# Two layer ends reordered: squares of the last tile summed second, first root turned early, first weight chunks in halves

## What is computed

```
h = _rmsnorm(x, pre_g) * (1 + scale) + shift
proj = h @ w_in
...
x = x + gate * _rmsnorm(y @ w_out, post_g)
```

## Time and profile before

| what | value |
| --- | --- |
| device time, median of 3 runs | 2637.5 us (2636.26 to 2640.43) |
| the profiled execution's own time | 2639.43 us |
| its span | 2637.6 us |
| TensorE's mean granted clock | 0.981 of full |
| instructions | 31436 |
| DVE busy | 1608.5 us (61%) |
| ACT busy | 944.1 us (36%) |
| POOL busy | 131.8 us (5%) |
| HBM | 147 GB/s over the span |

### The profile page before, as it was taken

The page is one execution under the profiler, slowest core; times in us unless marked ns, Lnnn a source line. Parts: engine busy times, 40 slices in busy tenths (PEclk is TensorE's granted clock), DMA queues, the critical chain, the costliest instruction groups (busy, mean ns, idle before and its releaser), DMA issues.

```text
span 2637.6 us, 31436 instructions
## 1 busy us (share of the span) xinstructions
PE 2571.3 (97%) x12691; PEld 2078.8 (79%) x12691; DVE 1608.5 (61%) x2400; ACT 944.1 (36%) x1502; POOL 131.8 (5%) x121
## 2 busy tenths in 40 slices
PE   7999999999999999999999998999999999999998
PEld 4779777777777878888877887787888878878786
DVE  4445666677777768676697757668455534445432
ACT  4222444434444324331334333444344323223321
POOL 0000000000001103001021102000000000000000
PEclk8999999999999989999999998999999999999999
DMA  9934433344447635655657554454222223322432
GB/s 350 341 121 146 128 112 112 112 128 128 128 128 240 207 127 184 202 185 175 212 167 262 178 159 156 143 160 128 80 73 87 86 80 92 92 88 90 155 111 72
DMA packets 301074, 390.67 MB, mean 148 GB/s; under 512 B 11698, under 2 KB 237618, under 8 KB 297090
## 3 DMA queue, kind: packets, MB, share of 16 engines
q1 hardware_dynamic: 294800, 354.79, 42.9%
q0 software_dynamic: 6128, 33.89, 3.4%
q10 hardware_dynamic: 2, 0.00, 0.0%
HBM read 371.85 MB, written 16.78 MB: 147 GB/s over the span
## 4 chain that ended last, share of the span: by engine, by line
PE 87%; DVE 6%; DMA 2%; issue 2%; ACT 2%; SPq 1%; POOL 0%; ACTq 0%; DVEq 0%; POOLq 0%
PE G L1849 72%; PE OB L1849 5%; PE S L1849 5%; PE TB L1849 2%; PE TB L1852 2%; DVE MACC L1387 2%; DMA LATE<-in_ev_mod_w 1%; DMA MRAW<-in_ev_mod_w 1%; DVE WLO L1381 1%; DVE Y L1381 1%; SPq L927 0%; PE OB L1852 0%; DMA MORE<-in_ev_mod_w 0%; DVE SQ L1387 0%; ACT WHI L1056 0%
## 5 line engine op out<-in xcount | busy, mean ns | idle before, releaser
L1849 PE MATMUL G<-HHI,WHI 128*128 128x512 f32 x2624 | 1107.5, 422 | 25.4 <-issue 7.7
L1849 PE MATMUL G<-HHI,WLO 128*128 128x512 f32 x2624 | 1032.9, 394 | 0.0
L1849 PE MATMUL G<-HLO,WHI 128*128 128x512 f32 x2624 | 1030.6, 393 | 0.0
L1381 DVE TENSOR_TENSOR WLO<-RAW,WHI 128x1024 fp32r<-128x1024 f32 x376 | 464.3, 1237 | 331.1 <-ACT WHI L1056 328.2
L1849 PEld LDWEIGHTS G<-HHI,WHI 128*128 128x128 f32 x2624 | 497.3, 190 | 144.4 <-issue 31.5
L1056 ACT ACTIVATE WHI<-RAW 128x1024 fp32r<-128x1024 f32 x376 | 395.7, 1054 | 587.3 <-PE G L1849 534.5
L1849 PEld LDWEIGHTS G<-HLO,WHI 128*128 128x128 f32 x2624 | 498.4, 190 | 113.1 <-issue 17.0
L1849 PEld LDWEIGHTS G<-HHI,WLO 128*128 128x128 f32 x2624 | 496.9, 189 | 109.5
L1387 DVE SCALAR_TENSOR_TENSOR MACC<-MWIDE,SC,MACC 128x512 f32<-128x512 f32 x420 | 340.0, 810 | 23.4 <-DMA MWIDE<-in_w_ada 9.6
L1849 PE MATMUL G<-WHI,HHI 128*128 128x256 f32 x640 | 186.5, 291 | 0.0
L1849 PE MATMUL G<-WLO,HHI 128*128 128x256 f32 x640 | 181.0, 283 | 0.0
(11 more groups left out here) (270 smaller groups left out, 2367.2 us busy)
## 6 DMA issues: line engine op xcount, KB each, us to landing
RAW<-in_w_in SPq DMA_DIRECT2D x128, 512.0 KB, 3.8
MWIDE<-in_od_mod_w SPq DMA_DIRECT2D x96, 512.0 KB, 4.7
MWIDE<-in_w_ada SPq DMA_DIRECT2D x96, 512.0 KB, 4.6
RAW<-in_ev_w_in SPq DMA_DIRECT2D x80, 512.0 KB, 3.6
RAW<-in_od_w_in SPq DMA_DIRECT2D x64, 512.0 KB, 3.8
MWIDE<-in_ev_mod_w SPq DMA_DIRECT2D x32, 512.0 KB, 4.5
RAW<-in_ev_w_out SPq DMA_DIRECT2D x32, 512.0 KB, 4.1
RAW<-in_od_w_out SPq DMA_DIRECT2D x32, 512.0 KB, 4.0
```

Of the source, the lines that this page charges most:

```text
L1381: return e.o.tensor_tensor(o, a, b, op)
L1849: return e.o.matmul(o, l, r, start=start, stop=stop, skip_group_check=True)
```

## The change

The squares of tile 15 are summed directly behind those of tile 14. The sums of XY and YSQ of tile 15 go behind the turn of the first root. The first x_add comes in front of n_rstd and the second behind it. The multiplications of tiles 4 and 5 move from in front of pair 2 to behind it. The gain is formed at the start of o_rstd. The first two chunks are run in halves: both chunks' tiles k = 0 and 1, then both chunks' tiles 2 and 3. And PE waits for HHI (signal a_h) before the first matmul of a tile and for HLO only before the second.

```diff
 gemm_dual
-            for c in range(8):
-                i = at["use"]
-                at["use"] += 1
+            i0 = at["use"]
+            at["use"] += 8
+            while at["split"] <= i0 + 1:
+                split_next()
+            halves = [(0, 0), (1, 0), (0, 1), (1, 1)] + [(c, jj) for c in range(2, 8) for jj in range(2)]
+            for c, jj in halves:
+                i = i0 + c
                 while at["split"] <= i:
                     split_next()
-                for jj in range(2):
-                    for nt in range(2):
-                        put("mm2", "h", layer, u, i, c % 2, c // 2 * 4, nt, jj, (first + c) % 2)
-                    next(tiles, None)
-                while at["split"] < min(i + NS, len(chunks)):
+                for nt in range(2):
+                    put("mm2", "h", layer, u, i, c % 2, c // 2 * 4, nt, jj, (first + c) % 2)
+                next(tiles, None)
+                while jj and at["split"] < min(i + NS, len(chunks)):
                     split_next()
...
 project_out
+                if layer < 3 and uu == 7:
+                    for x, k in ((0, 14), (0, 15), (1, 14), (2, 14)):
+                        put("o_tail", layer, x, k)
...
 next_layer
             put("o_rstd", layer - 1)
+            put("o_tail", layer - 1, 1, 15)
+            put("o_tail", layer - 1, 2, 15)
+            put("x_add", layer - 1, 0)
             put("n_rstd", layer)
+            put("x_add", layer - 1, 1)
...
-                    for j in ((0, 1), (2, 3, 4, 5))[k // 2] if k < 4 else (k + 2, k + 3):
+                    for j in ((), (2, 3), (4, 5, 6, 7))[k // 2] if k < 6 else (k + 2, k + 3):
...
 dve_program, o_rstd (and the same lines gone from the end of n_rstd)
+                e.wait_ge(v_mod, (11, 23)[layer - 1])
+                g = MOD[:, layer, 16:32]
+                gain = COL[:, 80:96] if layer == 1 else COL[:, 112:128]
+                stt(g, g, 1.0, gain, ADD, MUL).then_inc(*v_intro.up(("gain", layer + 1)))
...
 pe_program
-        def split_mm(o, wh, wl, hi, lo, start, stop):
+        def split_mm(o, wh, wl, hi, lo, start, stop, low=None):
             mm(o, wh, hi, start, False)
+            if low:
+                e.wait_ge(*low)
             mm(o, wh, lo, False, False)
...
-                    e.wait_ge(ready, key)
+                    if kind == "h":
+                        e.wait_ge(a_h, ("t", layer, k))
+                    else:
+                        e.wait_ge(ready, key)
...
-                    t = split_mm(G[pair][nt][:, :], wh[:, j, cols], wl[:, j, cols], hi, lo, k == 0, k == 15)
+                    t = split_mm(G[pair][nt][:, :], wh[:, j, cols], wl[:, j, cols], hi, lo, k == 0, k == 15, (ready, key))
...
+            elif stage == "o_tail":
+                layer, x, k = a
+                done, key = ((a_sqy, (layer, k)), (v_xy, (layer, k)), (a_sq, ("e", layer, k)))[x]
+                e.wait_ge(done, key)
+                t = token_sums(x, (SQ4[k % 4], XY[k % 2], YSQ[k % 2])[x], False)
+                if k == 15 and x != 1:
+                    t.then_inc(*p_stat.up(("o", layer, k) if x == 0 else ("m", layer + 1)))
```

More of the change, by code:

```diff
@@ L1693, in dve_program @@
                 stt(ROOT2, t, 1.5, y, ADD, MUL).then_inc(*v_rs.up((("n", layer), 4)))
[L1694 to L1697, removed]
             elif stage == "x_add":
@@ L2093, in pe_program @@
                 gf[pair][nt] = (a_ev, ("o", layer, k)) if layer < 3 else (v_res, k)
-                if layer < 3 and k >= 14:
-                    e.wait_ge(a_sqy, (layer, k))
-                    token_sums(0, SQ4[k % 4], False).then_inc(*p_stat.up(("o", layer, k)))
             elif stage == "o_sums":
```

## The result

The changed kernel takes 2647.72 us (median of 7 runs, 2641.37 to 2651.82) against 2637.5 us (7 runs, 2634.31 to 2641.1). The ratio is 1.0031, 95% interval 1.0021 to 1.0041: slower by some 8 us (the two medians by themselves differ by 10.2), where 2633.4 was forecast and 2636.9 was the upper end of the range. The profiled execution took 2647.72 us with a span of 2645.8 us.

What follows compares the result with a forecast made beforehand. PE, busy 97% of the span, bounds the kernel; only its waits or low clock can be won. Gains of 1.65 + 3.25 = 4.9 us at the two layer ends; middle of 2632.6 and 2634.2 taken: 2633.4 us, range 2630.7 to 2636.9.

Steps and rivals of the forecast that it cites:

- What is late next: Layer ends, up to tile 11: DVE sets the gain; the 113th matmul starts 1.65 us earlier, 3.25 at the second end.
- The sequel: Low clock behind a PE wait at a layer end: 3.4 us of it costs some 1.6 us.
- The front term: Roots before the new layer's first matmul: SQ begins 0.45 us earlier (0.31 to 0.50).
- my two prices: PE time for turning the first root ahead of the last sums: 1.09 or 0.86 us; 0.95 taken.
- The first matmuls and the halves: New layer's start: first matmul some 1.3 us earlier, tile 2's 1.56 us wait gone, PE 2.1 us ahead.
- the second slow stretch: Second layer end, behind the wait for tile 2: low clock for 3.4 us, costing some 1.6 us, goes.
- POOL takes DVE's time: Rival at pair 4: HLO also waits for POOL's fourth addition, 1.25 us later; 2635.1, up to 2637; chance 0.20.
- the slower one: Rival, low halves of pairs 4 to 10: POOL's full additions cost 3.5 us at tile 11; 2644.3; chance 0.05.

Runs made afterwards that it cites:

- e1: Changed kernel with the third weight chunk split early, between the first x_add and the second root: 2632.98 us, ratio 0.9981 to the kernel before.
- e2: Changed kernel with the third chunk split at its old place, behind pair 4 and ahead of pair 6's multiplications: 2634.71 us, ratio 0.9990 to the kernel before.
- e4: Kernel before with only the halves added, the third chunk split behind pair 6 as in the change: 2645.25 us, ratio 1.0026.
- e5: Kernel before with the halves, and the third chunk split early, ahead of n_rstd (the second root): 2631.86 us, ratio 0.9979.
- e7: Kernel before with only the later wait for HLO, so PE starts on HHI: 2639.5 us, ratio 1.0004.
- e3: Changed kernel with chunks whole and PE waiting for HLO at once, leaving front part and x_add order: 2634.41 us, ratio 0.9984 to the kernel before.
- e8: Changed kernel with the third chunk split before the first x_add and multiplications of tiles 4 and 5 ahead of the second root: 2631.3 us, ratio 0.9976.
- e9: Changed kernel with early third-chunk split and only tile 4's multiplication ahead of the second root, tile 5's with tiles 2 and 3: 2628.29 us, ratio 0.9961.

## Why the prediction was wrong

**The step that failed** is a sentence under "What is late next": "The fourth chunk's WLO, now behind pair 6, is made at 1000.6 and needed at 1002.3". The time at which it is made was nearly right: 1001.0 in the changed kernel, whose layer end began 0.35 us sooner, so 0.75 us later than forecast. The chunk was wrong. gemm_dual splits up to chunk i + 3, not including it, when it has used chunk i, and the units before do the same. So as the new layer begins only its first two chunks are split. WLO_71 and WLO_72, which I called the fourth and fifth chunk under "The change" too, are the third and fourth. PE needs WLO_71 for the 49th matmul, by my own count of positions at 996.8, not for the 73rd at 1002.3. In the kernel before this split stood ahead of pair 6, with slack. Its WLO was made from 995.74 to 996.96, and the 49th matmul began at 999.06:

```profile
995.74 1.21 DVE L1381 TENSOR_TENSOR WLO<-RAW,WHI 128x1024 fp32r<-128x1024 f32 x1
```

```profile
999.06 0.39 PE L1849 MATMUL G<-HHI,WHI 128*128 128x512 f32 x1
```

The order rows of the change show the move; I read it and gave it the wrong consumer. e1, e2, e4 and e5 show that this is all of the loss.

**The sequel** was also left out: the slow stretch behind a long wait, which I had priced at 1.6 us for 3.4 us of low clock, lasted 6.3 us of PE's work behind a wait of 5.6 us and cost 3 us at each end.

**The front term** had the right sign and was too small: 0.45 us forecast. SQ of pair 0 began 12.42 us behind the last projection matmul before, and 11.69 in the changed kernel: 0.73 us earlier. The second root began 0.67 us later (8.33 us behind the last projection matmul instead of 7.66), not 0.95. The rows of PE for the turn ahead of the last sums:

```profile
972.79 0.87 PE L1863 MATMUL TB<-IDN,COL 128*128 128x128 f32 x4
973.46 1.70 PE L1860 MATMUL S<-ONE,XY 128*128 128x1 f32 x8
```

It held PE for 973.46 - 972.79 = 0.67 us, below 0.86, the lower of my two prices, as part of it ran at the full clock. (By the price of 0.86 the term would have been 0.54 us, not the 0.50 that the prediction gives.) At the second end SQ began 12.96 and 11.69 us behind that matmul, 1.27 us earlier. Part of this is luck of the clock. In the kernel before it fell to half 3.3 and 2.8 us behind the last projection matmul, in the changed one some 4.5 us at both ends, so more of the sums ran at full speed. Over all ends of the kernels with the old front (before, e4 to e7), SQ begins 12.4 to 13.2 us behind that matmul, and in those with the front of the change (changed, e1 to e3) 11.7 to 12.7.

**The first matmuls and the halves** did what was forecast. The first matmul came 1.5 us sooner (1.3 forecast), no wait stood ahead of the 25th, and the second slow stretch behind the wait for tile 2 disappeared. That the start on HHI is worth nothing by itself (e7) was not said: it only lengthens the next wait, unless the halves fill it.

**POOL takes DVE's time**, the first rival, came true in part beside the main loss. HLO of pair 4 (both tiles, then tile 5 alone) and POOL's fourth addition in the changed kernel:

```profile
992.75 2.74 DVE L1398 SCALAR_TENSOR_TENSOR HLO<-SQ,MOD,HHI 128x512 fp32r<-128x512 f32 x2
```

```profile
993.71 1.78 DVE L1398 SCALAR_TENSOR_TENSOR HLO<-SQ,MOD,HHI 128x512 fp32r<-128x512 f32 x1
```

```profile
993.20 1.75 POOL L956 TENSOR_TENSOR Y<-Y,XR 128x512 f32<-128x512 f32 x1
```

The two HLO took 2.74 us, not the 1.42 of pair 2 nor the 1.76 of a pair beside additions, and the addition 1.75 instead of 1.26. HLO of tile 4 got in between the third and the fourth addition, as I had assumed, and took 1.04 us. HLO of tile 5, which I had not counted, waited for the fourth and ended 0.55 us behind it. Up to HLO of tile 4 DVE was 0.9 us ahead of the kernel before (24.17 against 25.08 us behind the last projection matmul); by the end of tile 5's it was level (26.9 in both). HLO of tile 11 ended 1012.19 - 968.58 = 43.6 us behind the last projection matmul, as before (1012.57 - 968.93 = 43.6), where I had it 0.8 us earlier. So even without the late chunk the gain at the first end is less than forecast: in e2 0.5 us at the 113th matmul instead of 1.65. At the second end it is 2.8 us instead of 3.25; the slow stretch of the kernel before, 1.6 us by my price, is gone there. e2's ratio of 0.9990 stands for 2.6 us; 4.1 were forecast for the change.

**Which rival decided:** the slower one that I wrote was about POOL and did not happen at that size. The one that happened, a wait for a weight chunk, I had excluded by the wrong count.

## What to carry to other kernels

When work is reordered by halves, everything that was timed by whole chunks moves with it: list for each engine what stands behind the new order, find the first consumer by counting positions from the loop's own bounds, and check the count against one row of the trace (here: the 49th matmul and the first WLO). If a producer has a pause ahead of the critical stretch, put the next weight chunk's preparation there. And when two measures shorten the same wait, test each alone: here the halves with the chunk in time gave 0.9979, the front alone 0.9984, and both together 0.9981, three results whose intervals overlap.

## What the runs showed of the hardware

A DVE operation on 128x4 elements with two inputs in SBUF took 1216 ns beside POOL's addition, where the same operation takes 161 to 163 ns without one (e8, e9). At the second end of e8 it took 1003 ns. In both cases it ended within 0.02 us of the end of the addition. The two operations in front of it, which read one input from PSUM (S), took 162 and 163 ns beside POOL's additions. The Trainium skill, page "SBUF — State Buffer", section "Who interferes with whom", has this as an exclusive lock against a DVE operation with two SBUF inputs; the rows agree, and they show that the price falls on a tiny operation in a chain of roots as much as on a large one. Where both engines had a row of such operations, they took turns: in the changed kernel HLO of tile 4 ran between the third and the fourth addition, and HLO of tile 5 behind the fourth, so the fourth addition took 1.75 us and that HLO 1.78.

One-column matmuls keep PE busy by the profile, and yet here the low clock followed them. In the kernel before PE goes from dense matmuls to 24 entries of sums (962.15 to 964.74) and back without a pause. The stretch behind them, from 965.58 to 968.99, has PE busy for all 3.41 us at a granted clock of 0.52 (columns: us, PE busy us (count), granted clock, DMA share, GB/s). At the second end the like stretch, 1569.54 to 1572.95, has 0.51.

```profile
965.58:968.99 3.41, 3.41 (x10) 0.52 0.00 0
```
